# Attention by pairs of heads: 64-row scores of both heads, joint transposes and products, row sums applied to the output

## The reference, cut to what matters

```
q = q.reshape(B, nc, CHUNK, RPA_HEADS, RPA_HEAD_DIM) * (RPA_HEAD_DIM ** -0.5)
...
s = jnp.einsum('bihd,bjhd->bhij', q_c, k_c).astype(jnp.float32) + bias
valid = (c * CHUNK - pad + band_pos) >= 0
p = jax.nn.softmax(jnp.where(valid, s, NEG_INF), axis=-1)
return jnp.einsum('bhij,bjhd->bihd', p.astype(v_c.dtype), v_c)
...
return o @ w_out
```

## Time and profile before

| | |
|---|---|
| median of three executions | 1230.86 us |
| the profiled execution | 1229.79 us |
| its span | 1228.1 us |
| PE busy | 1197.0 us (97%), 5662 matmuls |
| DVE, ACT, POOL busy | 444.7, 450.8, 524.8 us |
| mean granted clock of PE | 0.995 |
| attention of layer 1, first scores to the last head's products | 652.2 to 819.6 us |

### The profile page before, as it was taken

How to read it: one execution, slowest core, us unless ns; L and a number is a source line. 1 busy time by engine, 2 the same in 40 slices (tenths; PEclk the granted TensorE clock), 3 DMA queues, 4 the chain that set the end, 5 groups by cost and what they waited for, 6 DMA issues and landing times.

```text
span 1228.1 us, 14978 instructions
## 1 busy us (share of the span) xinstructions
PE 1197.0 (97%) x5662; PEld 994.1 (81%) x5662; DVE 444.7 (36%) x739; ACT 450.8 (37%) x708; POOL 524.8 (43%) x286
## 2 busy tenths in 40 slices
PE   8999999999999999999999989889999999999997
PEld 7888778988888888888887777678988888888886
DVE  4041272632222221001517898965322222220005
ACT  4372144233223222122427777752423223222111
POOL 4438316154444444446243333363344444444441
PEclk9999999999999999999999999989999999999999
DMA  5523303152222222224022212131222222222211
GB/s 209 195 100 134 103 1 138 48 193 102 85 86 102 102 102 101 77 97 171 19 104 76 78 44 86 43 138 69 97 76 101 102 102 102 83 88 104 103 69 68
DMA packets 22110, 119.76 MB, mean 98 GB/s; under 512 B 2464, under 2 KB 6944, under 8 KB 9136
## 3 DMA queue, kind: packets, MB, share of 16 engines
q1 hardware_dynamic: 16304, 107.06, 24.2%
q10 hardware_dynamic: 5760, 12.07, 2.8%
HBM read 117.02 MB, written 5.24 MB: 100 GB/s over the span
## 4 chain that ended last, share of the span: by engine, by line
PE 86%; DVE 10%; ACT 2%; issue 1%; DMA 1%; SPq 0%; POOL 0%; DVEq 0%; POOLq 0%; ACTq 0%
PE bank L1202 27%; PE bank L1204 27%; PE bank L1203 27%; DVE s_r_p L1134 2%; DVE s_neg_max L1124 2%; DVE bank L1120 2%; DVE s_pt_lo L1139 1%; PE bank L1264 1%; PE bank L1401 1%; PE bank L1410 1%; DVE s_r_k_lo L1102 1%; DVE s_r_q L1108 1%; DVE s_r_o L1149 1%; ACT s_r_k_hi L647 1%; PE bank L1442 1%
## 5 line engine op out<-in xcount | busy, mean ns | idle before, releaser
L768 POOL TENSOR_TENSOR s_w_lo<-s_raw,s_w_hi 128x1024 fp32r<-128x1024 f32 x183 | 440.3, 2411 | 528.9 <-ACT s_w_hi L443 528.9
L443 ACT ACTIVATE s_w_hi<-s_raw 128x1024 fp32r<-128x1024 f32 x183 | 192.1, 1057 | 398.2 <-PE bank L1204 375.4
L1202 PE MATMUL bank<-s_t_hi,s_w_hi 128*128 128x512 f32 x832 | 325.0, 391 | 0.0
L1203 PE MATMUL bank<-s_t_lo,s_w_hi 128*128 128x512 f32 x832 | 324.1, 390 | 0.0
L1204 PE MATMUL bank<-s_t_hi,s_w_lo 128*128 128x512 f32 x832 | 324.1, 390 | 0.0
L1204 PEld LDWEIGHTS bank<-s_t_hi,s_w_lo 128*128 128x128 f32 x832 | 156.3, 188 | 32.8
L1203 PEld LDWEIGHTS bank<-s_t_lo,s_w_hi 128*128 128x128 f32 x832 | 156.4, 188 | 31.1
L1202 PEld LDWEIGHTS bank<-s_t_hi,s_w_hi 128*128 128x128 f32 x832 | 156.4, 188 | 31.0
L1202 PE MATMUL bank<-s_w_hi,s_a_hi 128*128 128x512 f32 x352 | 137.1, 390 | 0.0
L1204 PE MATMUL bank<-s_w_hi,s_a_lo 128*128 128x512 f32 x352 | 137.0, 389 | 0.0
L1203 PE MATMUL bank<-s_w_lo,s_a_hi 128*128 128x512 f32 x352 | 136.9, 389 | 0.0
(11 more groups left out here) (150 smaller groups left out, 1308.6 us busy)
## 6 DMA issues: line engine op xcount, KB each, us to landing
s_raw<-stream SPq DMA_DIRECT2D x97, 1024.0 KB, 4.8
s_ln_gb<-ln_gb ACTq DMA_DIRECT2D x4, 1024.0 KB, 4.8
bias_rows<-rel_bias ACTq DMA_DIRECT2D x1, 3072.0 KB, 13.1
s_h<-x ACTq DMA_DIRECT2D x1, 2048.0 KB, 12.7
s_r_b<-bias_rows ACTq DMA_DIRECT2D x16, 128.0 KB, 3.5
s_x_t<-x_t SPq DMA_DIRECT2D x3, 512.0 KB, 9.9
out<-s_h SPq DMA_DIRECT2D x3, 512.0 KB, 2.6
s_raw<-stream SPq DMA_DIRECT2D x2, 256.0 KB, 4.4
```

Source lines behind the costliest of these rows:

```text
L443: nc.scalar.activation(w_parts(n, slice(0, SLAB))[0], raw[:, pair % RAWS, n % 2, :], ACT.Copy).then_inc(hi_done, 2 if n == 1 else 1)
L768: nc.gpsimd.tensor_tensor(lo, raw[:, place // 2 % RAWS, n % 2, :], hi.bitcast(F32), ALU.subtract).then_inc(lo_done, 2 if n == 1 else 1)
L1202: nc.tensor.matmul(out, l_hi, r_hi, start=start, stop=False, skip_group_check=skip)
L1203: nc.tensor.matmul(out, l_hi, r_lo, start=False, stop=False, skip_group_check=skip)
```

## The change

The work goes by steps: a step is one query tile of both heads of a pair, 4 steps a pair, 32 in all. `unit(s)` now maps unit `s` to pair, tile and head.

- Scores: q and k are kept as they come, both heads in one 128-row tile with a high and a low part each (`q_hi`, `q_lo`, `k_hi`, `k_lo`), so the splits are one 128x512 instruction on each engine where there were two to four of 64x512. The scores of a head are three matmuls over its own 64 rows, and the two heads' matmuls alternate: 6 matmuls a step. q is negated, so the scores are too.
- Bias and maximum are one DVE instruction over all keys (`tensor_tensor_reduce`, add and minimum of the negated scores), with a bias tile widened to 512 keys with zeros. ACT takes exp of the negative.
- The weights are not scaled. The 8 row sums of a pair are inverted at once, ACT spreads them to 64 columns each (`spread_inverse`), PE transposes the result in 4 blocks into bank 6 (`turn_inverse`), and DVE multiplies the pair's output with it (`scale_heads`), one step of the loop after the head sums.
- Transposes of both heads' units of a tile follow each other, and so do the products with v of both heads (in the second step of the next pair, after both heads are complete).
- The loops of all engines are rewritten by steps; the pieces are spread (5, 2, 5, 4), with 4 ahead of the first step, and the parts of the output projection are laid by `LAST_PARTS`. In the last steps `pair_high` and the early slabs are placed anew: POOL splits the first early slab after four pairs' outputs and the other three after all seven.

```diff
+            def q_high(p):
                 act.wait_ge(slab_done, RPA_KQ + 2 * p + 2)
...
+                nc.scalar.activation(r_qk[p % 2]["q_hi"][:, :], bank[1][:, :], ACT.Copy, scale=-(RPA_D ** -0.5)).then_inc(q_hi_done, 1)
...
+            def spread_inverse(p):
+
+                act.wait_ge(inverted, p + 1)
+                if p >= 1:
+                    act.wait_ge(inv_turned, p)
+                units = inv_sum[:, p * PAIR_UNITS:(p + 1) * PAIR_UNITS]
+                nc.scalar.activation(inv_wide[:, :, :], units.unsqueeze(2).to_broadcast([P, PAIR_UNITS, RPA_D]), ACT.Copy
+                                     ).then_inc(inv_spread, 1)
...
+            for step in range(UNITS // 2):
+                p, t = step // TILES, step % TILES
                 ahead = p + 1 < RPA_PAIRS
+                if ahead and t == 1:
+                    k_high(p + 1)
+                if ahead and t == 3:
+                    q_high(p + 1)
+                if t == 1:
+                    exponents(2 * step)
+                    exponents(2 * step + 1)
+                if step >= 1:
+                    weights_high(2 * step - 2)
+                    weights_high(2 * step - 1)
+                if t != 1:
+                    exponents(2 * step)
+                    exponents(2 * step + 1)
...
             load_gb(2)
+            spread_inverse(RPA_PAIRS - 1)
             head_half(RPA_HEADS - 2)
-            last_pair_high(0)
             head_half(RPA_HEADS - 1)
-            last_pair_high(1)
+            pair_high(RPA_PAIRS - 2)
+            split_hi(FFN_IN[1] + 2)
+            split_hi(FFN_IN[1] + 3)
+            pair_high(RPA_PAIRS - 1)
             out_projection(RPA_OUT, KD, 2)
...
             for p in range(RPA_PAIRS - 1):
                 pool.wait_ge(o_hi, p + 1)
...
-                if p == 1:
+                if p == 3:
                     split_lo(FFN_IN[1])
-                if p == RPA_PAIRS - 3:
-                    pool.wait_ge(s_done, UNITS)
-                    split_lo(FFN_IN[1] + 1)
-            split_lo(FFN_IN[1] + 2)
-            pool.wait_ge(o_lo, 3)
-            split_lo(FFN_IN[1] + 3)
+            for n in range(1, TAIL):
+                if n == TAIL - 1:
+                    pool.wait_ge(o_lo, RPA_PAIRS // 2)
+                split_lo(FFN_IN[1] + n)
...
+            def bias_and_max(s):
...
+                blk = bank[2 + hd][:, 0:keys]
+                nc.vector.tensor_tensor_reduce(out=blk, in0=blk, in1=r_b[:, p % 2, hd, SEQ - keys:], scale=1.0, scalar=-NEG_INF,
+                                               op0=ALU.add, op1=ALU.min, accum_out=neg_max[:, s:s + 1]).then_inc(s_biased, 1)
...
+            for step in range(UNITS // 2):
+                p, t = step // TILES, step % TILES
+                bias_and_max(2 * step)
+                bias_and_max(2 * step + 1)
+                if p >= 1 and t == 0:
+                    invert_sums(p - 1)
+                if step >= 1:
+                    weights_low(2 * step - 2)
+                    weights_low(2 * step - 1)
+                if p + 1 < RPA_PAIRS and t == 1:
+                    k_low(p + 1)
+                if p + 1 < RPA_PAIRS and t == 3:
+                    q_low(p + 1)
+                if p >= 1 and t == 2:
+                    head_sum(2 * p - 2)
+                    head_sum(2 * p - 1)
+                if p >= 1 and t == 3:
+                    scale_heads(p - 1)
...
+                if s >= 2:
+                    pe.wait_ge(exp_done, s)
+                qk = r_qk[p % 2]
+                terms = [("q_hi", "k_hi"), ("q_hi", "k_lo"), ("q_lo", "k_hi")]
+                for i, (q, k) in enumerate(terms):
+                    for hd in range(2):
+                        rows = own_half(hd)
+                        last = nc.tensor.matmul(bank[2 + hd][:, keys], qk[q][rows, toks], qk[k][rows, keys],
+                                                start=(i == 0), stop=(i == 2))
...
+            PIECES = (5, 2, 5, 4)
+            LEAD = 4
+            LAST_PARTS = ((0, 1), (2,), (3, 4, 5), (6, 7))
...
+            for step in range(UNITS // 2):
+                p, t = step // TILES, step % TILES
+                scores(2 * step)
+                if step >= 1:
+                    turn_weights(2 * step - 2)
+                    turn_weights(2 * step - 1)
+                if p >= 1 and t == 3:
+                    turn_inverse(p - 1)
+                if p >= 1 and t == 1:
+                    weights_v(2 * p - 2)
+                    weights_v(2 * p - 1)
+                for piece in pieces[done:done + PIECES[t]]:
+                    kq_piece(*piece)
```

More of the change, by code:

```diff
@@ L346, in build_program @@
         o_lo = sem("o_lo")
-        last_hi = sem("last_hi")
         last_lo = sem("last_lo")
@@ new lines, in pair_high, with exponents @@
+                act.wait_ge(o_scaled, p + 1)
+                nc.scalar.activation(t_hi[:, p, :], r_o[p][:, :], ACT.Copy).then_inc(o_hi, 1)
+            def exponents(s):
+                _, t, hd = unit(s)
+                act.wait_ge(s_biased, s + 1)
+                if s >= 4:
+                    act.wait_ge(p_turned, s - 3)
+                nc.scalar.activation(r_p[:, s % 4, 0:(t + 1) * P], bank[2 + hd][:, 0:(t + 1) * P], ACT.Exp,
+                                     bias=neg_max[:, s:s + 1], scale=-1.0, accum_out=row_sum[:, s:s + 1]).then_inc(exp_done, 1)
@@ L1558, in _ @@
                 kq_piece(*piece)
+            done = LEAD
             pe.wait_ge(v_lo_done, 2 * TILES)
[L1560 to L1589 removed]
```

332 lines of the change are left out of this document (137 added, 195 removed).

## The result

The changed kernel took 1222.55 us (median of 4 executions, 1221.52 to 1223.68), the kernel before 1230.34 in the runs beside it: a ratio of 0.9939, 95% interval 0.9927 to 0.995. It is faster, by 7.8 us where 12.75 were forecast. The profiled execution took 1223.68 us, 6.1 less than the one shown of before.

The account below looks back on a forecast made before the run. DVE was taken to set the pace in the attention pairs, PE elsewhere. From 1229.8 us, +0.7, -1.35, -10.5, -4.8, +2.7 and +0.5 total -12.75: 1217.0, or 1218.0 for a median; range 1213 to 1228.

Parts of the forecast that it names:

- two rivals: Weight loads of the two row halves follow each other (1223.4, chance 0.20); fused instruction at half speed (1226.8, chance 0.12).
- DVE bounded the kernel and would no longer: Ordinary pairs: DVE sets the pace, busy 18.45 of 20.5 us; after the change 11.7 us, no longer the bound.
- The fused instruction: DVE's bias and minimum with accumulator: 8 a pair at 0.56 us, 4.5 us; at worst 8.4.
- The rival of half speed: Fused instruction at half speed: DVE's chain in the fourth step 5.6 us, 8.8 in all, 1226.8; chance 0.12.
- The row halves overlap: PE's six score matmuls a tile run beside each other in two row halves: three slots, 1.92 us.
- rivals of serial weight loads: Score matmuls of both halves cost 0.11 us each at least: +0.7 a pair, 5.4 in all, 1223.4; chance 0.20.
- of no overlap: Six score matmuls of a step run alone, each alternation paid: PE's need 22.5 us a pair, 1244 to 1246; chance 0.08.
- Entry and exit of a 64-row group, 0.75 us a pair: PE's scores: 0.16 to 0.2 us extra for each group, four times a pair, taken from layer 0.
- Every step closes in time: Scores wait for both heads' previous exponents; longest step: DVE done about 4.2 us, PE needs 4.7; allowance 0.5 us.
- First and last pair: First pair 16.3 us instead of 17.65, -1.35; last pair, up to the last head's products, -4.8 from 25.47.
- The wait for POOL's low slabs, +2.7: Behind the last pair: last slabs fetched only after the early slabs are done; PE waits about 2.7 us.
- Everywhere else nothing changes: Outside the pairs where DVE sets the pace, PE is the bound and the change touches nothing; start put at 0.

Follow-up runs that it names:

- joint group: Changed kernel with the scores of a pair's first two tiles in one 64-row group, and high slabs made earlier on ACT: 1216.57 us, ratio 0.988.
- 128-row run: Changed kernel with two score matmuls over all 128 rows for each head instead of three over 64, numerically wrong: 1218.43 us, ratio 0.9904.
- reordering: Changed kernel with ACT splitting the seventh pair's output before the last head halves, and the third and fourth early slab behind the last weights: 1220.41 us, ratio 0.9919.

## Why the prediction was right, and where its size was off

The mechanism was right and the gain too large: 7.8 us (medians) where 12.75 were forecast. The 1222.55 us lie outside the 4 us to either side of the forecast itself, and inside the range only because it was drawn out to 1228 for two rivals. Both of these fell. That the first of them named 1223.4, close to what came out, is coincidence.

*DVE bounded the kernel and would no longer.* Right: 10.6 us busy in an ordinary pair, forecast 11.7. The run without scaling shows that this relief is the gain of an ordinary pair, and the run with an extra instruction that slack is left. That the scaling was "dearer than its size" was seen but not explained; the last section shows what it shared its time with.

*The fused instruction.* The row taken for it (L897) was a fair neighbour: 0.51 + 0.135 us against 0.56, which cost nothing, since DVE waits. The rival of half speed falls.

*The row halves overlap.* Right, mostly to 3 to 6 ns; the rivals of serial weight loads (a 128-key slot is 0.11 us for both heads: 729.56 to 729.67) and of no overlap fall.

*Entry and exit of a 64-row group, 0.75 us a pair.* **This step failed, by size.** I had 0.16 to 0.2 us a group from layer 0, by taking 0.216 for a product alone. But I measured there from the first 64-row start to the next 128-row start, and the price reaches beyond both. In the second group of the earlier trace rows the last product before it takes 0.31 us until the first 64-row start (153.02 to 153.33) where its neighbours take 0.216, and the first transpose behind takes 0.165 where the next take 0.109: 0.15 us more. The joint group shows 0.31, the 128-row run 0.355. That is 1.2 to 1.4 us a pair; PE's need came to 19.47 instead of 19.0, 2.8 us over six pairs. The seventh pair gave 0.6 of it back, which leaves the 2.2 us by which pairs two to seven missed. The Trainium skill, "TensorEngine Tiling (Array Packing)", Key Properties, has a change of tiling mode drain the array. The size in the trace agrees: by that rule I had worked out 0.5 us more a pair, and set it aside for the layer 0 rows; 0.47 more was measured. That the array drains no row shows.

*Every step closes in time.* Right in the middle: no wait for exponents or for q's low part in pairs two to six. In the seventh pair's last step, which has no piece, it does not close, as foreseen: from its last matmul to the next pair's scores it is 2.1 us (785.9 to 788.0), ended by q's low part. That pair took 0.84 us less than the others, forecast 0.2.

*First and last pair.* -2.0 for -1.35 and -4.5 for -4.8. The last one holds some of the clock: PE was at its lower level for 6.8 us of it before and for 3.4 after (granted 0.87 and 0.92), and in the run with the heads one after the other, where it never fell, the last pair took 20.40 us instead of 21.01. How much of the 4.5 us that makes was not separated.

*The wait for POOL's low slabs, +2.7.* The queue was right, the size and the fetch that binds were not: four waits, one for each of the last slabs, with 3.5 us more between starts than the pieces need, and 4.5 in the stage with the four transposes of the inverse and the slow matmul behind. Forecast was one wait, for the last pair of slabs, fetched when all three early slabs were done. The one that bound was the pair before it, fetched when the first of the three was done (815.66 us) and landed 6.1 us later, not 4.8; and POOL needs 2.35 us for a slab where PE uses one in 1.4, so each of the four is late anew. The reordering gave 4.0 us of it back.

*Everywhere else nothing changes.* **This step failed too**, by 3.4 us, half of what is missing: the start was put at nothing. Its text is the same in both kernels, and from the 50th matmul on the distances are the same to 0.2 us, but in the changed kernel the first inputs land otherwise. ACT's first instructions in the kernel before, and then in the changed kernel:

```profile
4.74 0.63 ACT L523 ACTIVATE s_w_hi<-s_raw 128x512 fp32r<-128x512 f32 x1 [2.65 <-DMA s_raw<-stream]
5.30 0.81 ACT L525 ACTIVATE s_t_hi<-s_x_t 128x256 fp32r<-128x256 f32 x2
```

```profile
3.64 0.63 ACT L529 ACTIVATE s_w_hi<-s_raw 128x512 fp32r<-128x512 f32 x1 [1.56 <-DMA s_raw<-stream]
4.25 0.42 ACT L531 ACTIVATE s_t_hi<-s_x_t 128x256 fp32r<-128x256 f32 x1
6.57 0.42 ACT L531 ACTIVATE s_t_hi<-s_x_t 128x256 fp32r<-128x256 f32 x1 [1.90 <-DMA s_x_t<-x_t]
```

The first slab comes 1.1 us earlier, the second tile of x about 0.9 us later, and SP's issue of two later tiles takes 2.94 us instead of 1.20:

```profile
4.62 1.20 SPq L397 DMA_DIRECT2D s_x_t<-x_t  x2
```

```profile
4.66 2.94 SPq L401 DMA_DIRECT2D s_x_t<-x_t  x2
```

The other half is the clock. Up to the 40th matmul the changed kernel is 1.65 us late, by its inputs; then PE, which had waited 3.3 us from start to start for its inputs (12.23 to 15.56; before 2.1 us), was granted its lower level from 17.1 to 20.5 us, and eight matmuls 0.43 instead of 0.23 us apart made 1.6 us more. The kernel before, and then the changed one:

```profile
16.00:20.00 4.00, 4.00 (x19) 3.30 (x19) 4.00 (x2) 1.54 (x2) 4.00 (x2) 1.00 0.43 168
16.00:20.00 4.00, 4.00 (x14) 3.13 (x13) 2.98 (x2) 2.88 (x3) 4.00 (x2) 0.63 0.66 260
```

In three profiles of kernels built on the one before, the landmark comes at 173.0 to 173.3 us, and the clock never fell at the start. In eight built on the changed one it comes at 173.9 to 177.2: in four of them the clock fell there for 3.4 us (176.3 to 177.2), in four it did not (173.9 to 175.3). The first slab is 1.1 us earlier in all eight, and the issue takes 2.0 to 3.1 us in all eight. So it goes with the program, by an amount that differs from one to the next. The order of the issues is the same in both. What in the program does it was not tried, and stays open; the run with the extra VectorE instruction, at 173.9, shows that most of it can vanish by an unrelated edit.

In sum: of the 6.6 us missing between the profiles, 3.4 are the start, 2.2 pairs two to seven (the entries of the groups), 1.8 the end of the projection; the other terms take back 0.8.

## What to carry to other kernels

When one engine is relieved, ask what the freed time is spent on: here the joined 64-row scores paid an entry and exit of 0.31 to 0.36 us for each of the 32 steps, for a saved slot of 0.11 to 0.23, so wider groups (or plain 128-row operands, if the copies for them are cheap) are better. Lay the narrow products of several tiles into one group before anything else. And look at the ends of a software pipeline apart: order and slack that cost nothing in the steady state cost 0.4 to 4 us in the first and the last round. Last, compare stages from a common landmark, with the granted clock beside them: the start and the clock moved several of these totals by 1 to 4 us.

## What the runs showed of the hardware

- Products on two row halves of PE overlap in full with the halves in turn and with three of one half queued ahead of three of the other: pairs of 19.47 and 19.50 us. So they do not start in the order of the program. With eight queued ahead of eight (layer 0) eight of the sixteen overlapped.
- One group of 64-row products between 128-row ones costs 0.31 us (the joint group) to 0.355 us (the 128-row run) beyond its slots; within the group a change of width costs nothing visible.
- The fused bias-and-minimum instruction takes 0.30 to 0.73 us from 128 to 512 elements (mean 0.51), its accumulator 0.135.
- POOL holds up some instructions of DVE. The extra DVE instruction, two operands from SBUF, took 0.68 us or 1.87; its rows, and POOL's beside them:

```profile
737.22 0.68 DVE L1184 TENSOR_TENSOR s_spare<-s_causal 128x512 f32<-128x512 f32 x1
740.48 1.87 DVE L1184 TENSOR_TENSOR s_spare<-s_causal 128x512 f32<-128x512 f32 x1
```

```profile
739.38 2.41 POOL L781 TENSOR_TENSOR s_w_lo<-s_raw,s_w_hi 128x1024 fp32r<-128x1024 f32 x1 [1.16 <-ACT s_w_hi L451]
```

  Of its 31 instances the 17 that lie beside no POOL instruction are all fast (0.68 us). Eight take 1.49 to 1.87 us, and all eight lie for over 1.3 us beside POOL instructions that read two tensors. The other six lie beside POOL instructions that read one tensor, or only for 0.2 us beside one that reads two, and take 0.68 to 0.81 us. The removed scaling (`scale_weights`, SBUF to SBUF) is the same case in the kernel before: 0.28, 0.35, 0.41 and 0.48 us by width when fast, 1.56 us for 128 elements while POOL worked (766.34 to 768.73), 2.68 for 512:

```profile
764.83 0.48 DVE L1134 TENSOR_SCALAR s_r_p<-s_r_p,s_inv_sum 128x512 f32<-128x512 f32 x1
767.26 1.56 DVE L1134 TENSOR_SCALAR s_r_p<-s_r_p,s_inv_sum 128x128 f32<-128x128 f32 x1
```

```profile
766.34 2.39 POOL L768 TENSOR_TENSOR s_w_lo<-s_raw,s_w_hi 128x1024 fp32r<-128x1024 f32 x1 [2.05 <-ACT s_w_hi L443]
```

  Of its 64 instances 18 are slow, all beside POOL, none of the 31 beside no POOL instruction; the excess is 16.8 us over all. In these pairs POOL's own instruction never took over 0.1 us more than without one of DVE's beside it (2.39 to 2.48 us). In the pair of the earlier trace rows the excess of the scaling is 4.9 - 3.0 = 1.9 us, about what PE lost there. DVE instructions with an operand from a bank (the fused one, L1140) never show it: the fused one takes 0.73 us at most, L1140 0.69. So the change took the division off a DVE instruction that POOL could hold up, and multiplies with a bank operand instead (L1155, 0.68 us). The Trainium skill, "GPSIMD Engine Reference", Specifications, says that GpSimd's SBUF interfaces are shared with VectorE, with contention for instructions in a 2-port mode or with two SBUF inputs. The trace agrees for the extra instruction, which has two SBUF inputs; the scaling has one and is slow beside POOL too, but no row shows the mode that it ran in. No run took the overlap away by itself, so its share of the gain is read from the rows, not tested.
- Two programs with the same text at their start can reach the same matmul 1 to 4 us apart, part by their first inputs, part by the clock. Where a kernel was profiled twice, the two agreed to 0.2 us (before) and 0.5 us (changed).
- Up to the end of the attention PE's lower clock level was granted in stretches of 3.4 or 6.8 us, mostly after it had stood waiting: at 689.1 us before, behind 2.3 us from start to start (686.5 to 688.8), and at 788.5 in the changed kernel, behind 2.1. Such a wait alone does not decide it: the later pairs of the kernel before have the same 2.3 us at the full clock, and in the run with the transposes first PE waited 3.3 us at the start without a fall.
